# Forgetting attention on one core: where silu of the gate runs, and where ScalarE loads its function table

## The chip, the cores and the metric

The kernel runs on one core of a Trainium2 chip. A core has TensorE (PE in the profile, with its weight loads as PEld), VectorE (DVE), ScalarE (ACT), GpSimd (POOL) and a queue engine that issues transfers (SP). The metric is device time in microseconds. Before the change it was 2946.18 us, the median of three runs (2945.17 to 2953.4).

## The reference, cut to what matters

The program is a first block of two layers, followed by a second block of two mixers. The last mixer is forgetting attention over 512 positions with 16 heads of 64, and this change is inside it:

```python
def fox_mixer(h, w_in, f_bias, qn_w, kn_w, w_out):
    proj = h @ w_in
    q, k, v, z, f = jnp.split(proj, [...], axis=-1)
    q = rmsnorm(q.reshape(shp), qn_w) * FOX_HEAD_DIM ** -0.5
    k = rmsnorm(k.reshape(shp), kn_w)
    log_f = jax.nn.log_sigmoid(f + f_bias)
    cum = jnp.cumsum(log_f, axis=1)
    o = forgetting_attention(q, k, v, cum).reshape(B, S, FOX_WIDTH)
    o = o * jax.nn.silu(z)
    return o.astype(h.dtype) @ w_out

def forgetting_attention(q, k, v, cum):   # for each block of 128 queries
    logits = jnp.einsum('bqhd,bkhd->bhqk', q_b, k)
    logits = logits + (c_b[..., :, None] - cum_k[..., None, :])
    p = jax.nn.softmax(jnp.where(mask, logits, -jnp.inf), axis=-1)
    return jnp.einsum('bhqk,bkhd->bqhd', p, v)
```

So each pair of heads needs four projections (q, k, v, z) of 1024 by 128, two root mean square norms, a causal softmax, its product with v, and a product with silu(z).

## The kernel before, in words

Activations lie transposed (features on partitions, 512 positions in a row). Every weight block (1024 by 128) is loaded in float32, rounded by ScalarE into `w_hi` (L237), and its rest is formed by VectorE in `w_lo` (L243). A projection of one block is 24 products on TensorE (L255), three for each of 8 slices of the depth.

Forgetting attention handles two heads in a **turn**, eight turns in all, numbered 0 to 7 here. `fox_turns` writes turns 0 to 5 as a loop of three trips with two turns each, and turns 6 and 7 behind it. A turn has 16 steps n, and each engine has its own hand-written order of them. In the same steps the projections and norms of the **next** pair are made (`fox_next_pe`, `fox_next_act`, `fox_next_dve`), so that turn j also prepares turn j+1. Turn 7 has no next pair; it mixes in products of the output projection (L2608 to L2610) instead. The preparation of turn 0 stands alone ahead of the loop. Engines meet only through semaphores, and each engine executes its own list strictly in that order.

What stands in the steps:

- n = 0 to 7: TensorE makes the scores of unit n, s0 to s7 (L2564 to L2566, two heads times four query blocks); VectorE takes the row maximum (L2707, L2709); ScalarE computes ex0 to ex7, the exponentials with the row sums (L2644); VectorE inverts the sums (L2697) and GpSimd scales the probabilities (L2731). The scores of unit u wait for exponential u-2, which frees the bank.
- n = 8 to 15: TensorE transposes the probabilities, t0 to t7 (L2574); ScalarE copies each result out of the bank, pc0 to pc7 (L2652); TensorE multiplies it with v, v0 to v7 (L2582), one step later.
- Every n: a quarter of a projection of the next pair (six products, L255). At n = 7 and n = 10 TensorE also sums squares of q and of k with a product with ones (L2457), which waits for ScalarE's squares (L2472, at n = 5 and n = 9).
- ScalarE for the next pair: `w_hi` at n = 0, 4, 8, 12; at n = 8 the logarithm and exponential that give the inverse root for q (L2478, L2480), at n = 11 the same for k; at n = 10 four half copies of q (L2487, L2490), at n = 13 two of k (L2495), at n = 15 a copy of the turned v (L2498).
- The end of a turn: VectorE multiplies the attention with silu(z) (L2703, after v3 and v7), ScalarE rounds the product into `h_hi` (L2659), VectorE forms `h_lo` (L2718).

ScalarE computes nonlinear functions from a loaded table set. Silu needs another set than the exponential and the logarithm, and the compiler puts an ACT_TABLE_LOAD ahead of a function that the present set lacks; `preload_act_table_set` puts one where it is written. Copies and squares need none. In the kernel before, silu of the present pair's z stands right behind pc0 (L2655), and ahead of each of the two logarithms stands a preload of the set that has logarithm and exponential (L2476).

Of the kernel before, what the change touches and what calls it, by code (L numbers as in the profile page):

```python
# [108 lines left out]
def first_and_second_block(nc, a, out):  # L109

    with ExitStack() as ctx:
        def sem(name):
            return ctx.enter_context(nc.semaphore(name))
# [589 lines left out]
        class Gla:  # L703
# [3 lines left out]
            u = [tile(f"gla_u{n}", (21, 30, 31, 32)[n]) for n in range(4)]  # L707
# [14 lines left out]
            act = Steps(sem("gla_act"), ["zb0", "az0", "zb1", "az1", "ez0", "ez1", "lz0", "lz1"]  # L722
                        + [f"{n}{m}" for m in range(2) for n in ("eq", "ek", "e_mid", "e_all", "e_end")]
                        + ["vt0", "vt1", "kt0", "kt1", "vt2", "vt3"] + [f"{n}{h}" for p in (0, 2) for n in ("sq", "oc", "ln") for h in (p, p + 1)] + [f"rs{h}" for h in range(4)]
                        + [f"silu{h}" for h in range(4)] + ["hi7", "hi6", "hi5", "hi4", "hi0", "hi1", "hi2", "hi3"])
# [406 lines left out]
        class Dsa:  # L1132
# [23 lines left out]
            act = Steps(sem("dsa_act"), ["sin1", "abs1", "cos1", "sin0", "abs0", "cos0"]  # L1156
                        + [n for d in range(12) for n in [f"rl{d + 1}{h}" for h in range(IDX_HEADS) if d < TT - 1]
                           + [f"sw_{r}" for r in dsa_swaps[d]]] + ["vt0", "vt1", "vt2", "vt3"])
# [6 lines left out]
        class DsaAtt:  # L1165

            units, groups = range(DSA_UNITS), range(DSA_UNITS // DSA_GROUP)
# [3 lines left out]
            act = Steps(sem("dsa_att_act"), [f"ex{u}" for u in range(2)]  # L1171
                        + [n for u in units for n in [f"ex{u + 2}"] * (u + 2 < DSA_UNITS) + [f"pc{u}"]
                           + [f"hi{u // DSA_GROUP - 1}"] * (u >= DSA_GROUP and u % DSA_GROUP == 1)] + [f"hi{DSA_UNITS // DSA_GROUP - 1}"])
# [354 lines left out]
        class Gdn:  # L1528
# [12 lines left out]
            zs = [tile(f"gdn_zs{h}", 18 + h) for h in range(2)]  # L1541
# [6 lines left out]
            XT, X, F, m, V1, F2, V, CY = Pw[0], Pw[1], W2[0], W2[1], W3[1], W5[0], W5[1], W3[0]  # L1548
# [3 lines left out]
            raw, x, ax, ex = W1[0], W2[0], W3[0], Pw[0]  # L1552
# [48 lines left out]
        class GdnNext:  # L1601

            pe = Steps(sem("gdn_next_pe"), ["sum_q", "sum_k"])
            act = Steps(sem("gdn_next_act"), ["cw0", "cw1", "cs0", "cw2", "cs1", "sq_q", "sq_k", "cw3", "ss_q", "ss_k", "cs2", "cs3",
                                              "ln_q", "ln_k", "rs_q", "rs_k", "eg_0", "eg_1", "dec_0", "dec_1"])
# [3 lines left out]
        class GdnOut:  # L1609

            act = Steps(sem("gdn_out_act"), both(["ln", "rs", "hi"]))
            dve = Steps(sem("gdn_out_dve"), both(["on", "o", "lo"]))

        class GdnTurn:
# [7 lines left out]
            act = Steps(sem("gdn_act"), ["kc", "vc_0", "vc_1", "fa", "fb", "c", "f2a", "y", "bt", "ct"]  # L1622
                        + [n for t in range(TT) for n in both([f"vn{t}"])] + both(["sq", "oc"]))
# [746 lines left out]
        class Fox:  # L2370
            b0, t0 = BASE["fox"]
            f, x, ax, ex, all_ones, cum = (tile(f"fox_{n}", 31 + k) for k, n in enumerate(("f", "x", "ax", "ex", "all_ones", "cum")))
# [20 lines left out]
        class FoxTurn:  # L2393

            units = range(2 * TT)
            pe = Steps(sem("fox_turn_pe"), [f"s{u}" for u in units] + [n for u in units for n in [f"t{u}"] + [f"v{u - 1}"] * (u > 0)] + ["v7"])
            act = Steps(sem("fox_turn_act"), [f"ex{u}" for u in units] + [n for u in units for n in [f"pc{u}"] + ["zs"] * (u == 0)] + ["hi"], 2 * 8 + 2)
            dve = Steps(sem("fox_turn_dve"), [n for u in units for n in [f"mx{u}", f"nm{u}"] + [f"ri{u - 1}"] * (u > 0)] + ["ri7", "ga_0", "ga_1", "lo"], 1)
            pool = Steps(sem("fox_turn_pool"), [f"pn{u}" for u in units])

# [63 lines left out]
        def fox_next_act(act, n, j, m, i, scored):  # L2464

            F, N = Fox, FoxNext
            if n % 4 == 0:
                split_hi(act, fox_block(m, n // 4) + AHEAD, i, 8)
            if n in (5, 9):
                k = (5, 9).index(n)  # L2470
                act.wait_ge(*fox_taken(m, k, i))
                act.activation(F.sq[k][:], (F.q, F.k)[k][:], ACT.Square).then_inc(*N.act.done(f"sq_{'qk'[k]}"))  # L2472
            if n in (8, 11):

                k = (8, 11).index(n)
                act.preload_act_table_set("natural_log_exp_and_others")  # L2476
                act.wait_ge(*N.pe.after(f"sum_{'qk'[k]}", j))
                act.activation(F.sd[k][:], fox_bank(m, k)[:], ACT.Ln, bias=eps_c, scale=1.0 / FOX_DH).then_inc(*N.act.done(f"ln_{'qk'[k]}"))  # L2478
                act.wait_ge(*N.act.after(f"ln_{'qk'[k]}", j))
                act.activation(F.sd[k][:], F.sd[k][:], ACT.Exp, scale=-0.5).then_inc(*N.act.done(f"rs_{'qk'[k]}"))  # L2480
            if n == 10:
                act.wait_ge(*N.dve.after("n_q", j))
                if scored:
                    act.wait_ge(*scored)
                for h in range(2):
                    r = fox_rows(h)[0]
                    act.activation(F.q2[h][r, :], F.q[r, :], ACT.Copy).then_inc(*N.act.done(f"q2_{h}"))  # L2487
                for h in range(2):
                    r, other = fox_rows(h)
                    act.activation(F.q2[h][other, :], F.q[r, :], ACT.Copy).then_inc(*N.act.done(f"qq_{h}"))  # L2490
            if n == 13:
                act.wait_ge(*N.dve.after("n_k", j))
                for h in range(2):
                    r = fox_rows(h)[0]
                    act.activation(F.k2[h][r, :], F.k[r, :], ACT.Copy).then_inc(*N.act.done(f"k2_{h}"))  # L2495
            if n == 15:
                act.wait_ge(*N.pe.after("vt", j))
                act.activation(F.v_tok[m % 2][:], fox_bank(m, 2)[:], ACT.Copy).then_inc(*N.act.done("vt"))  # L2498
# [121 lines left out]
        def fox_act(act, after):  # L2620
            F, N, H, s = Fox, FoxNext, FoxTurn, Fox.act
            act.sem_inc(H.act.sem, H.act.lead)
            project_act(act, F.b0, 1)
            act.wait_ge(tile_free, BANKS + F.t0 + 1)
            r = slice(0, P)
            act.activation(F.x[r, :], F.f[r, :], ACT.Identity, bias=nfox_b[r, :]).then_inc(*s.done("x"))
            act.activation(F.ax[r, :], F.f[r, :], ACT.Abs, bias=nfox_b[r, :]).then_inc(*s.done("ax"))
            act.wait_ge(*s.after("ax"))
            act.preload_act_table_set("natural_log_exp_and_others")
            act.activation(F.ex[r, :], F.ax[r, :], ACT.Exp, scale=-1.0).then_inc(*s.done("ex"))  # L2630
            act.wait_ge(*s.after("ex"))
            act.activation(F.ax[r, :], F.ex[r, :], ACT.Ln, bias=1.0).then_inc(*s.done("ln"))
            for n in range(16):
                if n == 8:
                    act.wait_ge(*F.dve.after("ones"))
                fox_next_act(act, n, 0, 0, 0, None)

            def turn(j, i, m, last):
                for n in range(16):
                    if not last and n < 8:  # L2640
                        fox_next_act(act, n, j + 1, m + 1, i, H.pe.after("s7", j))
                    if n < 8:
                        act.wait_ge(*H.dve.after(f"nm{n}", j))
                        act.activation(fox_p(n), bank[4 + n % 2][:, 0:fox_keys(n)], ACT.Exp, bias=nmax[:, n:n + 1],  # L2644
                                       scale=FOX_DH ** -0.5, accum_out=rowsum[:, n:n + 1]).then_inc(*H.act.done(f"ex{n}"))
                    else:
                        u = n - 8
                        act.wait_ge(*H.pe.after(f"t{u}", j))
                        if u >= 2:
                            act.wait_ge(*H.pe.after(f"v{u - 2}", j))  # L2650
                        w = T - u % TT * P
                        act.activation(F.pT[u % 2][:, 0:w], bank[4 + u % 2][:, 0:w], ACT.Copy).then_inc(*H.act.done(f"pc{u}"))  # L2652
                        if u == 0:
                            act.wait_ge(*fox_taken(m, 3, i))
                            act.activation(F.z[m][:], F.z[m][:], ACT.Silu).then_inc(*H.act.done("zs"))  # L2655
                        if not last:
                            fox_next_act(act, n, j + 1, m + 1, i, H.pe.after("s7", j))
                act.wait_ge(*H.dve.after("ga_1", j))
                act.activation(h_hi[:, col(j)], F.gated[:], ACT.Copy).then_inc(*H.act.done("hi"))  # L2659
            fox_turns(act, turn)  # L2660
            down_act(act, F.b0 + FOX_P, KT, after)

# [399 lines left out]
```

## Time and profile before

| what | value |
|---|---|
| median of three runs | 2946.18 us |
| the profiled execution | 2946.31 us |
| its span, first to last instruction | 2944.5 us |
| mean granted TensorE clock | 0.981 |
| TensorE busy | 2813.8 us |
| VectorE busy | 1616.8 us |
| ScalarE busy | 1259.0 us |
| GpSimd busy | 621.9 us |

Times in rows are microseconds from the span's start. "Idle before <-releaser" in brackets is how long the engine stood still before the instruction, and what ended that. A granted clock of 1.00 is TensorE's full 2.4 GHz, 0.50 is 1.2 GHz. The preparation of turn 0 begins near 2570 us, turn 0 begins at 2600.60 us and the last turn ends near 2902 us; the output projection and the final norm follow.

### The profile page before, as it was taken

What the parts mean: (1) busy time and instruction counts of PE and PEld (TensorE: products, weight loads), DVE (VectorE), ACT (ScalarE), POOL (GpSimd) and SP (SyncE); (2) the same over time, 40 slices, a digit from 0 to 9 for tenths busy, and PEclk for the clock granted to TensorE, in tenths of its full rate; (3) what the DMA queues carried; (4) which work ended last, traced back from release to release, by engine and by line L of the source; (5) the groups of instructions that cost most, each with busy time, mean ns of one, the idle gap of its engine ahead of it and who ended that gap; (6) DMA issues with size and microseconds to landing.
All of it is one profiled execution on the core that took longest, in us unless ns stands there. A gap on an engine that the chain in (4) does not pass through costs nothing.

```text
span 2944.5 us, 41200 instructions
## 1 busy us (share of the span) xinstructions
PE 2813.8 (96%) x14333; PEld 2279.4 (77%) x14333; DVE 1616.8 (55%) x2484; ACT 1259.0 (43%) x1853; POOL 621.9 (21%) x594
## 2 busy tenths in 40 slices
PE   7999999999999999999899999979999999799998
PEld 5888877788888878886678788857888887576667
DVE  4444345544433665336845653266777777565554
ACT  4443242444422333233443332255555555466664
POOL 2000103100001550013533510233333333122222
PEclk9999999999999999999899999999999999899999
DMA  4333332233333563332114643321222222122212
GB/s 120 103 95 96 92 79 72 72 99 94 91 98 89 168 174 113 93 91 72 43 51 136 177 130 94 94 72 51 66 66 65 66 65 55 44 65 52 55 50 65
DMA packets 485303, 255.65 MB, mean 87 GB/s; under 512 B 18819, under 2 KB 479398, under 8 KB 485174
## 3 DMA queue, kind: packets, MB, share of 16 engines
q1 hardware_dynamic: 483856, 253.25, 30.1%
q8 instruction: 81, 1.33, 0.2%
q10 hardware_dynamic: 1318, 0.69, 0.1%
q14 instruction: 48, 0.39, 0.0%
HBM read 251.77 MB, written 2.13 MB: 86 GB/s over the span
## 4 chain that ended last, share of the span: by engine, by line
PE 76%; DVE 9%; ACT 5%; issue 4%; POOL 4%; ACTq 0%; DVEq 0%; DMA 0%; POOLq 0%
PE bank L255 58%; PE bank L1727 2%; ACT w_hi L237 2%; POOL sumsq L587 1%; PE bank L2582 1%; POOL ada_sum L587 1%; DVE dsa_work L1458 1%; DVE prod L683 1%; PE bank L1758 1%; DVE ada_hi L573 1%; PE bank L1825 1%; PE bank L1760 1%; PE bank L1759 1%; DVE w_lo L243 1%; DVE small L1456 1%
## 5 line engine op out<-in xcount | busy, mean ns | idle before, releaser
L255 PE MATMUL bank<-x_hi,w_hi 128*128 128x512 f32 x2328 | 958.4, 412 | 20.3 <-DVE w_lo L243 9.0
L255 PE MATMUL bank<-x_hi,w_lo 128*128 128x512 f32 x2328 | 915.4, 393 | 0.0
L255 PE MATMUL bank<-x_lo,w_hi 128*128 128x512 f32 x2328 | 914.5, 393 | 0.0
L243 DVE TENSOR_TENSOR w_lo<-w_raw,w_hi 128x1024 fp32r<-128x1024 f32 x430 | 550.2, 1281 | 661.8 <-ACT w_hi L237 655.1
L237 ACT ACTIVATE w_hi<-w_raw 128x1024 fp32r<-128x1024 f32 x430 | 451.1, 1052 | 426.5 <-PE bank L255 388.4
L255 PEld LDWEIGHTS bank<-x_hi,w_hi 128*128 128x128 f32 x2328 | 442.2, 190 | 131.3 <-issue 21.5
L255 PEld LDWEIGHTS bank<-x_hi,w_lo 128*128 128x128 f32 x2328 | 441.3, 190 | 95.6
L255 PEld LDWEIGHTS bank<-x_lo,w_hi 128*128 128x128 f32 x2328 | 442.7, 190 | 92.5 <-issue 9.1
L400 POOL TENSOR_TENSOR sumsq<-sumsq,sq 128x512 f32<-128x512 f32 x54 | 91.9, 1703 | 1318.5 <-ACT sq L386 1317.1
L255 PE MATMUL bank<-h_hi,w_hi 128*128 128x512 f32 x768 | 298.9, 389 | 1.6 <-DVE h_lo L1483 1.6
L255 PE MATMUL bank<-h_lo,w_hi 128*128 128x512 f32 x768 | 298.8, 389 | 0.0
L255 PE MATMUL bank<-h_hi,w_lo 128*128 128x512 f32 x768 | 298.8, 389 | 0.0
L659 ACT ACTIVATE h_hi<-prod 128x512 f32 x88 | 55.7, 632 | 387.9 <-DVE prod L683 387.9
L255 PEld LDWEIGHTS bank<-h_hi,w_hi 128*128 128x128 f32 x768 | 144.2, 188 | 31.8 <-issue 1.8
L255 PEld LDWEIGHTS bank<-h_hi,w_lo 128*128 128x128 f32 x768 | 144.2, 188 | 29.9
L255 PEld LDWEIGHTS bank<-h_lo,w_hi 128*128 128x128 f32 x768 | 144.2, 188 | 29.7
L656 ACT ACTIVATE gate_s<-gate_s 128x512 f32<-128x512 f32 x88 | 55.7, 632 | 184.5 <-DVE gate_s L675 184.5
L680 DVE TENSOR_TENSOR prod<-bank,rstd 128x512 f32<-128x512 f32 x88 | 60.6, 689 | 85.9 <-PE bank L255 85.9
L686 DVE TENSOR_TENSOR h_lo<-prod,h_hi 128x512 f32 x88 | 62.4, 709 | 82.3 <-ACT h_hi L659 82.3
L587 POOL TENSOR_TENSOR sumsq<-sumsq,ada_hi 128x512 f32<-128x512 f32 x48 | 62.1, 1294 | 159.9 <-DVE ada_hi L573 159.9
L2731 POOL TENSOR_TENSOR fox_p<-fox_p,small 128x128 f32<-128x128 f32 (+1 forms) x64 | 59.0, 921 | 99.4 <-DVE small L2697 98.6
L683 DVE TENSOR_TENSOR prod<-prod,gate_s 128x512 f32<-128x512 f32 x88 | 77.0, 875 | 4.6
(450 smaller groups left out, 3663.4 us busy)
## 6 DMA issues: line engine op xcount, KB each, us to landing
w_raw<-in_ffn_wi_dram SPq DMA_DIRECT2D x176, 512.0 KB, 3.8
w_raw<-in_ffn_wo_dram SPq DMA_DIRECT2D x64, 512.0 KB, 3.6
w_raw<-in_ada_w_dram SPq DMA_DIRECT2D x48, 512.0 KB, 4.8
w_raw<-in_a_w_in_dram SPq DMA_DIRECT2D x48, 512.0 KB, 3.9
w_raw<-in_b_w_in_dram SPq DMA_DIRECT2D x32, 512.0 KB, 4.0
w_raw<-in_ffn_wo_dram SPq DMA_DIRECT2D x32, 384.0 KB, 3.1
w_raw<-in_even_w_in_dram SPq DMA_DIRECT2D x16, 512.0 KB, 4.0
w_raw<-in_a_w_out_dram SPq DMA_DIRECT2D x16, 512.0 KB, 3.6
```

The costliest lines, as they stand in the source:

```text
L237: act.activation(w_hi[b % SPLIT][:], w_raw[raw % RAW][:], ACT.Copy).then_inc(w_hi_done, 1)
L243: dve.tensor_tensor(w_lo[s][:], w_raw[raw_of(b) % RAW][:], w_hi[s][:].bitcast(F32), ALU.subtract).then_inc(w_lo_done, 1)
L255: mm = pe.matmul(out, lhs[:, w], rhs(kt), start=first and kk == 0 and m == 0, stop=last and kk == len(kts) - 1 and m == 2)
L400: pool.tensor_tensor(sumsq[:], sumsq[:], sq[k % 2][:], ALU.add).then_inc(sum_added, 1)
L587: pool.tensor_tensor(dst, x, y, ALU.add).then_inc(ada_added, 1)
L656: act.activation(gate_s[s][:], gate_s[s][:], ACT.Silu).then_inc(silu_done, 1)
L659: act.activation(h_hi[:, col(i * 2 + 2 * turn0 + s)], prod[s][:], ACT.Copy).then_inc(h_hi_done, 1)
L680: dve.tensor_tensor(prod[s][:], bank[(t0 + o + 1) % BANKS][:], rstd[:], ALU.mult).then_inc(tile_free, 1)
L683: dve.tensor_tensor(prod[s][:], prod[s][:], gate_s[s][:], ALU.mult).then_inc(prod_done, 1)
L686: dve.tensor_tensor(h_lo[:, h], prod[s][:], h_hi[:, h].bitcast(F32), ALU.subtract).then_inc(h_ready, 1)
L1727: mm = pe.matmul(out[:, c * INV_PART:(c + 1) * INV_PART], lhs(c), rhs(c), start=True, stop=True)
L2731: pool.tensor_tensor(fox_p(u), fox_p(u), rinv[:, u:u + 1].to_broadcast([P, fox_keys(u)]), ALU.mult).then_inc(*H.pool.done(f"pn{u}"))
```

## The change

Two edits on ScalarE, and the list of its signals that goes with them. The preload inside `fox_next_act` is taken out, and one preload of the same set is written at the head of every turn. Silu of z moves from behind pc0 (n = 8) to behind pc5 (n = 13), and it now comes after that step's work for the next pair. What is computed stays the same.

```diff
-            act = Steps(sem("fox_turn_act"), [f"ex{u}" for u in units] + [n for u in units for n in [f"pc{u}"] + ["zs"] * (u == 0)] + ["hi"], 2 * 8 + 2)
+            act = Steps(sem("fox_turn_act"), [f"ex{u}" for u in units] + [n for u in units for n in [f"pc{u}"] + ["zs"] * (u == 5)] + ["hi"], 2 * 8 + 2)
...
                 k = (8, 11).index(n)
-                act.preload_act_table_set("natural_log_exp_and_others")
                 act.wait_ge(*N.pe.after(f"sum_{'qk'[k]}", j))
...
             def turn(j, i, m, last):
+
+                act.preload_act_table_set("natural_log_exp_and_others")
                 for n in range(16):
...
                         act.activation(F.pT[u % 2][:, 0:w], bank[4 + u % 2][:, 0:w], ACT.Copy).then_inc(*H.act.done(f"pc{u}"))
-                        if u == 0:
+                        if not last:
+                            fox_next_act(act, n, j + 1, m + 1, i, H.pe.after("s7", j))
+                        if u == 5:
                             act.wait_ge(*fox_taken(m, 3, i))
                             act.activation(F.z[m][:], F.z[m][:], ACT.Silu).then_inc(*H.act.done("zs"))
-                        if not last:
-                            fox_next_act(act, n, j + 1, m + 1, i, H.pe.after("s7", j))
```

Only ScalarE's list changes. In these rows `fox_pT` is a copy pc, `fox_sd` the logarithm and exponential of a norm, `fox_sq` a square, `fox_p` an exponential ex; ISA and REGISTER_ALU rows are bookkeeping of semaphores and loop counters. In the first turn of the loop's body, behind pc0 at n = 8, ScalarE's list held this before:

```order
L2655 ACT_TABLE_LOAD
L2655 ACTIVATE fox_z_255<-fox_z_255 128x512 [waits tile_free]
L235 REGISTER_ALU
L236 REGISTER_ALU [waits w_loaded0]
L237 ACTIVATE w_hi_56<-w_raw_52 128x1024 [waits block_done]
L2476 ACT_TABLE_LOAD
L2477 ISA
L2478 ACTIVATE fox_sd_261<-bank,small 128x512 [waits fox_next_pe]
L2479 ISA
L2480 ACTIVATE fox_sd_261<-fox_sd_261 128x512 [waits fox_next_act]
L2648 REGISTER_ALU
L2652 ACTIVATE fox_pT_266<-bank 128x384 [waits fox_turn_pe]
```

In the changed kernel, the same place beginning with pc0 itself:

```order
L2653 ACTIVATE fox_pT_265<-bank 128x512 [waits fox_turn_pe]
L235 REGISTER_ALU
L236 REGISTER_ALU [waits w_loaded0]
L237 ACTIVATE w_hi_56<-w_raw_52 128x1024 [waits block_done]
L2476 ISA
L2477 ACTIVATE fox_sd_261<-bank,small 128x512 [waits fox_next_pe]
L2478 ISA
L2479 ACTIVATE fox_sd_261<-fox_sd_261 128x512 [waits fox_next_act]
L2649 REGISTER_ALU
L2653 ACTIVATE fox_pT_266<-bank 128x384 [waits fox_turn_pe]
L2471 REGISTER_ALU
L2472 ACTIVATE fox_sq_260<-fox_k 128x512 [waits tile_free]
```

Both table loads and silu are gone from between pc0 and the square of k; the rest keeps its order.

At n = 13, behind the two half copies of k, the list went straight to pc6 before:

```order
L2495 ACTIVATE fox_k_0_248<-fox_k 64x512 [waits fox_next_dve]
L2495 ACTIVATE fox_k_1_249<-fox_k 64x512
L2648 REGISTER_ALU
L2650 REGISTER_ALU [waits fox_turn_pe]
L2652 ACTIVATE fox_pT_265<-bank 128x256 [waits fox_turn_pe]
L2648 REGISTER_ALU
```

In the changed kernel a table load and silu stand there:

```order
L2494 ACTIVATE fox_k_0_248<-fox_k 64x512 [waits fox_next_dve]
L2494 ACTIVATE fox_k_1_249<-fox_k 64x512
L2657 REGISTER_ALU
L2658 ACT_TABLE_LOAD
L2658 ACTIVATE fox_z_255<-fox_z_255 128x512 [waits tile_free]
L2649 REGISTER_ALU
L2651 REGISTER_ALU [waits fox_turn_pe]
L2653 ACTIVATE fox_pT_265<-bank 128x256 [waits fox_turn_pe]
```

The pair that left n = 8 comes back in front of pc6.

At the border of two turns, the rounding into `h_hi` was followed by `w_hi` and ex0 before:

```order
L2659 ISA [waits fox_turn_dve]
L2659 ACTIVATE h_hi<-fox_gated 128x512
L236 REGISTER_ALU [waits w_loaded2]
L237 ACTIVATE w_hi_58<-w_raw_54 128x1024 [waits block_done]
L2643 ISA
L2644 ACTIVATE fox_p_263,small<-bank,small 128x128 [waits fox_turn_dve]
```

In the changed kernel:

```order
L2660 ISA [waits fox_turn_dve]
L2660 ACTIVATE h_hi<-fox_gated 128x512
L2639 ACT_TABLE_LOAD
L236 REGISTER_ALU [waits w_loaded2]
L237 ACTIVATE w_hi_58<-w_raw_54 128x1024 [waits block_done]
L2644 ISA
L2645 ACTIVATE fox_p_263,small<-bank,small 128x128 [waits fox_turn_dve]
```

A table load now stands in front of `w_hi` and ex0 of the new turn. In a turn there were three loads, and there are now two; in the preparation of turn 0 the two loads of L2476 are gone, and turn 0 has one at its head.

## Rows read from the trace of the kernel before

**Rows 1.** The page, part 1: busy time, share of the span, instructions.

```profile
PE 2813.8 (96%) x14333; PEld 2279.4 (77%) x14333; DVE 1616.8 (55%) x2484; ACT 1259.0 (43%) x1853; POOL 621.9 (21%) x594
```

**Rows 2.** Waits from 2600 to 2902 us: total, times, longest.

```profile
PE bank L2457 <- ACT fox_sq L2472: 22.2, 7, 3.2
...
PEld bank L2582 <- ACT fox_pT L2652: 4.3, 12, 0.5
```

**Rows 3.** Timeline of TensorE: first score product of turns 0, 2, 3, 4, 7.

```profile
2600.60 0.32 PE L2564 MATMUL bank<-fox_k,fox_q 128*128 128x128 f32 x1 [1.13 <-DVE fox_k L2538]
...
2679.00 0.22 PE L2564 MATMUL bank<-fox_k,fox_q 128*128 128x128 f32 x1
...
2717.27 0.22 PE L2564 MATMUL bank<-fox_k,fox_q 128*128 128x128 f32 x1
...
2757.28 0.22 PE L2564 MATMUL bank<-fox_k,fox_q 128*128 128x128 f32 x1
...
2876.09 0.22 PE L2564 MATMUL bank<-fox_k,fox_q 128*128 128x128 f32 x1
```

**Rows 4.** Timeline of ScalarE in turn 2: start us, us, engine, line, operation.

```profile
2695.04 0.60 ACT L2652 ACTIVATE fox_pT<-bank 128x512 f32<-128x512 f32 x1 [0.18 <-PE bank L2574]
2695.66 1.28 ACT L2655 ACT_TABLE_LOAD   x1
2696.95 0.63 ACT L2655 ACTIVATE fox_z<-fox_z 128x512 f32<-128x512 f32 x1
2697.49 1.04 ACT L237 ACTIVATE w_hi<-w_raw 128x1024 fp32r<-128x1024 f32 x1
2698.55 1.28 ACT L2476 ACT_TABLE_LOAD   x1
2699.85 0.69 ACT L2478 ACTIVATE fox_sd<-bank,small 128x512 f32<-128x512 f32 x1
2700.57 0.63 ACT L2480 ACTIVATE fox_sd<-fox_sd 128x512 f32<-128x512 f32 x1
2701.10 0.47 ACT L2652 ACTIVATE fox_pT<-bank 128x384 f32<-128x384 f32 x1
2701.47 0.62 ACT L2472 ACTIVATE fox_sq<-fox_k 128x512 f32<-128x512 f32 x1
```

**Rows 5.** Timeline of TensorE in the same turn.

```profile
2698.57 0.39 PE L255 MATMUL bank<-x_hi,w_lo 128*128 128x512 f32 x1
...
2702.14 1.13 PE L2457 MATMUL bank<-fox_sq,ones 128*128 128x512 f32 x2 [3.18 <-ACT fox_sq L2472]
```

**Rows 6.** Windows of TensorE: stretch, length, busy (instructions), granted clock, DMA share, GB/s.

```profile
2663.00:2663.50 0.50, 0.50 (x3) 0.50 0.49 148
2702.50:2703.00 0.50, 0.50 (x2) 1.00 1.15 348
2857.50:2858.00 0.50, 0.00 (x0) 0.51 0.52 150
```

**Rows 7.** Timeline of ScalarE, later in turn 2.

```profile
2706.64 1.28 ACT L2476 ACT_TABLE_LOAD   x1
...
2713.11 0.38 ACT L2652 ACTIVATE fox_pT<-bank 128x256 f32<-128x256 f32 x1 [0.83 <-PE bank L2574]
```

**Rows 8.** Head of turn 3: ScalarE, then the third score product.

```profile
2717.04 0.63 ACT L2659 ACTIVATE h_hi<-fox_gated 128x512 f32 x1 [1.03 <-DVE fox_gated L2703]
...
2719.07 0.37 ACT L2644 ACTIVATE fox_p<-bank,small 128x128 f32<-128x128 f32 x1 [0.45 <-DVE small L2709]
...
2720.73 0.34 PE L2564 MATMUL bank<-fox_k,fox_q 128*128 128x384 f32 x1
```

**Rows 9.** Before turn 0: TensorE at the second sum, and VectorE.

```profile
2589.65 1.12 PE L2457 MATMUL bank<-fox_sq,ones 128*128 128x512 f32 x2 [1.68 <-ACT fox_sq L2472]
...
2587.10 1.21 DVE L243 TENSOR_TENSOR w_lo<-w_raw,w_hi 128x1024 fp32r<-128x1024 f32 x1
```

**Rows 10.** Last turn: TensorE at the second value product.

```profile
2891.89 0.91 PE L2582 MATMUL bank<-fox_pT,fox_v_tok 128*128 128x384 f32 x2 [0.22 <-ACT fox_pT L2652]
```

## The prediction

> **What bounds the kernel now.** I read the page first: TensorE is busy for 2813.8 us of a span of 2944.5 us [rows 1]. Busy is not the same as necessary, but it says that a change on ScalarE counts only where TensorE stands still for ScalarE. So the second view is the list of waits over the stretch of the eight turns. One line outweighs the others there: TensorE waited 7 times for a square before a sum of squares, 22.2 us in total, 3.2 us the longest [rows 2]. Seven is the number of turns that prepare a next pair. The next line is much smaller: 12 waits of the weight load for a copy pc, 4.3 us.
>
> Third, the timelines of the two engines in turn 2. TensorE starts the last of its six products of n = 10 at 2698.57 and the sum of squares of k at 2702.14 [rows 5]. A full-rate product is followed by the next start 0.23 us later, so the sum could have started at 2698.80: the delay is 3.34 us. ScalarE has no gap at all from pc0 (2695.04) to the square of k (2701.47 to 2702.09) [rows 4]. This is one chain of nine instructions, and the square is its last. Three of the nine are what this change takes out.
>
> Fourth, the length of the turns and the granted clock. The first score product of turn 2 starts at 2679.00, of turn 3 at 2717.27, of turn 4 at 2757.28 [rows 3]: turn 2 takes 38.27 us and turn 3 takes 40.01 us, with the same work. The clock explains it. After the wait in turn 1, TensorE is granted 0.50 (1.2 GHz) in a stretch in which it is busy throughout; in turn 2, after an equally long wait, it keeps 1.00; in turn 6 the clock falls while it still waits [rows 6]. What TensorE did before each fall was nothing, for some 3 us. Turns 0 to 6 take 2876.09 - 2600.60 = 275.49 us together. Seven at 38.27 would be 267.89, so the low clock costs 7.6 us over them.
>
> **The change, part by part.**
>
> Chain from pc0 to the square of k. Removed are a load and silu (2695.66 to w_hi at 2697.49) and a load (2698.55 to the logarithm at 2699.85) [rows 4]. Rebuilt from the same rows: instructions of ScalarE overlap by about 0.1 us, as the exponential at 2700.57 (0.63) and pc1 at 2701.10 do. w_hi then starts at 2695.04 + 0.60 - 0.10 = 2695.54, the logarithm 0.95 later at 2696.49, the exponential 0.72 later at 2697.21 (it keeps its wait for the logarithm), pc1 at 2697.74, the square at 2698.11, ending at 2698.73. TensorE wants it at 2698.80. So the wait goes whole, with 0.07 us to spare; I count 3.35 us a turn less about 0.05 for the semaphore, 3.3 us. Simple subtraction of the rows gives 1.83 + 1.30 = 3.13 us, and I keep that as the lower end. Over seven turns: 23.1 us (21.9 to 23.4).
>
> Can the earlier instructions start earlier? w_hi needs a weight block that has landed, and a buffer freed by the block that TensorE ended at n = 7, before pc0. The logarithm needs the sum over q, also of n = 7. pc1 needs t1, which TensorE does before n = 10. None of them is late.
>
> Low clock. If a 3.2 us wait is what lets the clock fall, no turn has one any more, and the 7.6 us come back. The ends are 0 and 7.6; I take 7.5, since outside these waits I see no fall inside the turns.
>
> Second load of L2476, at n = 11 (2706.64) [rows 7]. It delays the second logarithm and all behind it on ScalarE by 1.3 us, up to pc4. v4 is one of the 12 short waits for a copy, 4.3 / 12 = 0.36 us each [rows 2]. I take 0.3 us a turn, 2.1 us in seven; ends 0 and 4.3.
>
> Silu at n = 13. A load of 1.28 and silu of 0.63 now stand before pc6. Ahead of them ScalarE is 1.3 us earlier by the load that went, and pc6 waited 0.83 us for its transposes anyway [rows 7]. That is 2.1 us of lead against 1.9 us of new work, so pc6 is late by at most 0.3 us where a little of the lead is lost at pc4 and pc5. v6 comes a step later, after six products (6 x 0.23 = 1.4 us). Queued behind the pair are pc6, pc7 and the copy of v; the gate product on VectorE also waits for silu now, but it runs only after that engine's two subtractions for k. I take 0; the ends are 0 and 0.3 us a turn, 2 us.
>
> Load at the head of a turn. It stands between h_hi (2717.04) and w_hi, with ex0 behind (2719.07, after 0.45 us idle) [rows 8]. ex0 becomes late by 1.30 - 0.45 = 0.85 us. The one who waits is the third score product; it needs ex0, which ended with its row sum about 0.46 us after its start, at 2719.53, and it starts at 2720.73. Slack 1.2 us, use 0.85: nothing, with 0.35 to spare. VectorE's inverse of the first sum is pushed by some 0.4 us, and w_lo behind it. The ends are 0 and 0.5 us a turn, 3.5 us.
>
> The Trainium skill bears on this place. "ScalarE: Activation LUTs", section "What ACT_TABLE_LOAD costs", says that a switch of sets costs the load of about 1.28 us and a drain of about 1.38 us. The rows agree on the load and show no drain: 0.02 us lie between the end of pc0 and the load, and 0.01 between the load and silu [rows 4]. By that rule the sum would be some 7 us smaller (rival B); the measured rows decide, and I go by 1.3.
>
> Preparation of turn 0. Both loads of L2476 vanish. TensorE waited 1.68 us at the second sum [rows 9] and 1.13 us at the first score [rows 3], 2.8 us together, which bounds the gain. The first norm of q is not free to move by all of 1.3 us, because VectorE is in w_lo until 2588.31 (2587.10 + 1.21) [rows 9]; I take 2.2 us, ends 1.3 and 2.8. The load at the head of turn 0 falls where ScalarE idles.
>
> Turn 7. Without load and silu before pc1, its value product does not wait (0.22 us and its late start [rows 10]): 0.4 us, ends 0 and 0.5. Silu before pc6 here delays the first gate product, which is not the last.
>
> **Sum**: 23.1 + 7.5 + 2.1 + 2.2 + 0.4 = 35.3 us. The profiled execution took 2946.31 us, 0.13 above the median, so the time is 2946.3 - 35.3 = 2911.0 us. The work of a plain turn falls from 38.27 to about 34.7 us.
>
> **The rivals.**
>
> A, the clock falls anyway. Some other short stillness may be enough once turns are shorter, or the wait at 2902 near the end may now meet a fall. For: in the rows equal waits gave a fall in one turn and none in the next, so a fall is not decided by the wait alone. Against: the dense stretches never show one. Cost up to 7.5 us: 2918.5.
>
> B, a new wait at the head or at pc6. The loads stand before ex0 and before silu, and my slack at the head is only 0.35 us. If both ends of those terms come true: 3.5 + 2 = 5.5 us, 2916.5. The strongest form is that a switch costs the length of the load once more before it: ex0 is then 0.85 + 1.30 = 2.15 us late against a slack of 1.2, which is 0.95 x 7 = 6.7 us, 2917.7. Against it stand the 0.02 us between pc0 and its load [rows 4]. The page of the Trainium skill named above states this form.
>
> C, the sum of squares goes free only by half, since something else in its chain is late once ScalarE is early (the copy of k by VectorE, a weight block). 1.65 x 7 = 11.5 us less, and the low clock stays in about half the turns: about 2926.
>
> D, slower. The square is not what TensorE waits for: another input of the sum arrives at the same moment, and nothing is gained there. Then ScalarE's new load at the head and the pair at n = 13 are on the path of each turn: 8 x (1.30 + 1.91) = 25.7 us on top, 2972. It decides only if no slack exists at the head, where I read 1.2 us, and ScalarE stood without a gap up to the very square that released TensorE. The rows speak against both halves.
>
> E, the loads that were removed return, placed by the compiler, and nothing happens: 2946. The order of the built program shows two per turn instead of three, so this is nearly excluded.
>
> **How the numbers follow.** Forecast (2906 to 2916) 0.70; A 0.11; B 0.09; C 0.06; D 0.02; E 0.02. The time is 2911. The lower end of the range adds the favourable ends: 0.3 at the sums, 2.2 at the copies, 0.6 before turn 0 and a little shorter turns otherwise, 2906; 2905 stands. The upper end takes in A and B and part of their combination, 2922. Beyond lie C, D and E. This kernel's measurement tells about 0.3%, some 9 us, from no change. All of forecast, A, B and C are more than that below 2946: faster 0.96, same 0.02, slower 0.02.
>
> **What would show it.** In the profile after: the wait of L2457 for the square of k gone from the list of waits or below 0.3 us each; turns of about 34.7 us from first score to first score, all alike; granted clock 1.00 throughout turns 0 to 7; the third score product of a turn still without a wait; pc6 starting with little or no idle time and v6 not waiting. The forecast is wrong if turns still come in two lengths, if the third score waits for ex0, or if the sum of squares waits for more than 1 us.

## The result, and the profile after

The changed kernel takes 2911.57 us, the median of four runs (2910.64 to 2913.47). The kernel before takes 2948.44 us in the runs beside it (2945.17 to 2953.4). The ratio is 0.9874, with a 95% interval of 0.9861 to 0.9888: 1.26% faster. The prediction was 2911.0 us. The four runs of the kernel before lie in two groups (2945.17 and 2946.18; 2950.7 and 2953.4), so its median falls between them. The profiled execution from which the prediction subtracts, 2946.31 us, is of the lower group.

The profiled execution took 2910.64 us, with a span of 2908.8 us. Part 1 of its page:

```profile
PE 2801.8 (96%) x14333; PEld 2272.5 (78%) x14333; DVE 1611.7 (55%) x2484; ACT 1247.7 (43%) x1845; POOL 624.4 (21%) x594
```

ScalarE has eight instructions less, which are the loads (16 removed, 8 added) [rows 1]. TensorE has the same 14333 products and 12 us less busy time.

The first score products of turns 0, 2, 3, 4 and 7, which answer to [rows 3] (in this kernel the line is L2563), in the timeline of TensorE:

```profile
2595.87 0.32 PE L2563 MATMUL bank<-fox_k,fox_q 128*128 128x128 f32 x1 [0.40 <-DVE fox_k L2537]
...
2665.74 0.22 PE L2563 MATMUL bank<-fox_k,fox_q 128*128 128x128 f32 x1
...
2700.43 0.22 PE L2563 MATMUL bank<-fox_k,fox_q 128*128 128x128 f32 x1
...
2735.46 0.22 PE L2563 MATMUL bank<-fox_k,fox_q 128*128 128x128 f32 x1
...
2839.48 0.22 PE L2563 MATMUL bank<-fox_k,fox_q 128*128 128x128 f32 x1
```

Turn 2 takes 34.69 us (38.27 before), turn 3 35.03 us (40.01 before), and turns 0 to 6 together 243.61 us (275.49 before). The chain of turn 1 on ScalarE, which answers to [rows 4]:

```profile
2646.69 0.60 ACT L2653 ACTIVATE fox_pT<-bank 128x512 f32<-128x512 f32 x1 [0.19 <-PE bank L2573]
2647.19 1.05 ACT L237 ACTIVATE w_hi<-w_raw 128x1024 fp32r<-128x1024 f32 x1
2648.14 0.68 ACT L2477 ACTIVATE fox_sd<-bank,small 128x512 f32<-128x512 f32 x1
2648.85 0.63 ACT L2479 ACTIVATE fox_sd<-fox_sd 128x512 f32<-128x512 f32 x1
2649.39 0.47 ACT L2653 ACTIVATE fox_pT<-bank 128x384 f32<-128x384 f32 x1
2649.76 0.62 ACT L2472 ACTIVATE fox_sq<-fox_k 128x512 f32<-128x512 f32 x1
```

From pc0 to the end of the square of k it is now 3.69 us instead of 7.05. TensorE at the sum of squares, against [rows 5]:

```profile
2650.24 0.40 PE L255 MATMUL bank<-x_hi,w_lo 128*128 128x512 f32 x1
2650.47 1.09 PE L2457 MATMUL bank<-fox_sq,ones 128*128 128x512 f32 x2
```

The sum (L2457) starts 0.23 us after the last product: there is no wait. The list of waits from turn 0 to the end of turn 7, against [rows 2]:

```profile
PEld bank L2581 <- ACT fox_pT L2653: 3.1, 8, 0.4
...
PE bank L2607 <- DVE h_lo L2719: 2.2, 1, 2.2
...
PEld bank L2457 <- ACT fox_sq L2472: 1.6, 7, 0.2
```

The 22.2 us of TensorE's own waits at L2457 are gone; what is left there is 1.6 us at the weight load, mostly hidden. The granted clock over turns 0 to 6, and in a stretch right behind turn 7:

```profile
2595.87:2839.48 243.61, 243.26 (x1149) 1.00 0.23 61
...
2866.00:2866.50 0.50, 0.50 (x2) 0.50 0.00 0
```

The same view of the kernel before, over its turns 0 to 6:

```profile
2600.60:2876.09 275.49, 252.96 (x1149) 0.97 0.20 54
```

Before, TensorE was busy for 252.96 of 275.49 us at a mean clock of 0.97; now it is busy for 243.26 of 243.61 us at 1.00, with the same 1149 instructions. So the turns are now TensorE's own work. The second row of the first of these fences is new and tells of something else: behind the last turn TensorE waits 2.2 us for `h_lo` (L2607 in the waits), and the clock is 0.50 after it in this execution.

Where the 35.7 us between the two spans went, by the starts of the same instructions:

| stretch | before | after | difference |
|---|---|---|---|
| start to the first activation of forgetting attention (untouched code) | 2573.14 | 2570.59 | -2.55 |
| preparation of turn 0, to its first score | 27.46 | 25.28 | -2.18 |
| turns 0 to 6 | 275.49 | 243.61 | -31.88 |
| turn 7 to the end | 68.41 | 69.32 | +0.91 |

The first row is no effect of the change: over the fourteen profiles of this document, whose code is the same up to there, that point lies anywhere from 2570.25 to 2573.61, and in a later profile of the changed kernel at 2572.00. The last holds the low clock behind turn 7: in that later profile it stays at full clock, and the stretch is 67.89 us, 0.52 less than before. So what the change itself moves is 2.18 + 31.88 + 0.52 = 34.6 us at full clock behind turn 7, and 33.2 us with the low clock of this execution.

### The profile page after: what moved, and what is told of

It reads as the page before. It is cut to its first block, busy times and chain, and to the rows that moved or that the text cites. A ratio compares the mean times of both kernels' runs of the same rounds, so it can differ in the third digit from the quotient of the medians.

```text
span 2908.8 us, 41195 instructions
## 1 busy us (share of the span) xinstructions
PE 2801.8 (96%) x14333; PEld 2272.5 (78%) x14333; DVE 1611.7 (55%) x2484; ACT 1247.7 (43%) x1845; POOL 624.4 (21%) x594
## 4 chain that ended last, share of the span: by engine, by line
PE 78%; DVE 9%; ACT 4%; POOL 4%; issue 4%; ACTq 0%; DVEq 0%; DMA 0%; POOLq 0%
PE bank L255 59%; PE bank L1727 2%; ACT w_hi L237 2%; POOL sumsq L587 1%; PE bank L2581 1%; POOL ada_sum L587 1%; DVE dsa_work L1458 1%; DVE prod L683 1%; PE bank L1758 1%; DVE w_lo L243 1%; DVE ada_hi L573 1%; PE bank L1825 1%; PE bank L1760 1%; PE bank L1759 1%; DVE small L1456 1%
```

## Experiments: how much of the chain, and what the clock does

**The old loads stay, only silu leaves the chain.** In `fox_next_act` of the changed kernel:

```diff
                 k = (8, 11).index(n)
+                act.preload_act_table_set("natural_log_exp_and_others")
                 act.wait_ge(*N.pe.after(f"sum_{'qk'[k]}", j))
```

> The changed kernel with both old loads kept ahead of the logarithms (n = 8 and n = 11), so of the change only silu and its load have left the chain. My theory: each instruction in the chain from pc0 to the square of k delays TensorE by its own length. The load at n = 8 is back, so the sum of squares of k waits about 1.3 us in each of 7 turns, v4 and v6 wait 0.3 us each again, and the preparation of turn 0 loses 2.2 us: 9.1 + 4 + 2.2 = 15 us over the changed kernel's 2911.6, near 2926. The waits of 1.3 us leave the clock at 1.00. Rival A, the clock falls whatever the length of the wait: about 7 us more, 2933. Rival, silu alone was the whole change and the other loads were covered: 2912.

Measured: 2924.57 us (2923.45 to 2926.08), ratio to before 0.9931 (0.9914 to 0.9947). TensorE's waits for the square over turns 0 to 6, and the window over them:

```profile
PE bank L2457 <- ACT fox_sq L2472: 8.6, 7, 1.2
```

```profile
2601.07:2856.31 255.24, 246.32 (x1149) 1.00 0.21 58
```

The wait is 1.23 us in each of 7 turns: one load, at its own length. The clock stays at 1.00, so a wait of this length brings no low clock with it here. The preparation of turn 0 is back at 27.46 us. Both rivals fall, and the theory is off by 1.4 us: v4 comes 0.27 us late again, as expected, but v6 does not, which I had priced at 0.3 us a turn. Against the kernel before beside it (2944.88) it is 20.3 us less: taking silu with its load out of the chain is more than half of the gain, low clock included, and the other loads are the rest.

**Two and three loads in the chain.** Again in the changed kernel, in the turns that prepare a next pair; the kernel with two has the first two of these, that with three has all:

```diff
+                if n == 8 and scored:
+                    act.preload_act_table_set("natural_log_exp_and_others")
                 act.wait_ge(*N.pe.after(f"sum_{'qk'[k]}", j))
...
+                if n == 8 and scored:
+                    act.preload_act_table_set("natural_log_exp_and_others")
                 act.wait_ge(*N.act.after(f"ln_{'qk'[k]}", j))
                 act.activation(F.sd[k][:], F.sd[k][:], ACT.Exp, scale=-0.5)...
+                if n == 8 and scored:
+                    act.preload_act_table_set("natural_log_exp_and_others")
```

> The changed kernel with two extra table loads in the chain of n = 8, one ahead of the logarithm and one between it and the exponential, in the 7 turns that prepare a next pair. My theory: the wait for the square of k comes back with 2 x 1.3 - 0.05 = 2.5 us, and pc6 is some tenths late: 7 x 2.6 = 18 us, 2930, if the clock stays at 1.00. If waits of 2.5 us let the clock fall as those of 3.2 us did, up to 7 us more, 2937. Rival with a drain at each load (a load costs 2.6 us): 7 x 5.2 = 36 us, 2948.

> As the last one with a third extra load, between the exponential and pc1. My theory: a wait of 3.85 us in 7 turns, 27 us, 2939, and the clock falls after it in each turn or nearly each (before: 4 of 7 with waits of 3.2 us), 1.7 us each: 12 us more, 2951. If the falls had another cause than the wait, they stay away and it is 2939.

Measured: 2934.44 us with two (ratio 0.9967, 0.9955 to 0.998), between the two times I had given (2930 and 2937), and 2952.94 us with three (1.0028, 1.0017 to 1.0038), where I had 2951. With two:

```profile
PE bank L2457 <- ACT fox_sq L2472: 17.5, 7, 2.5
```

```profile
2597.64:2863.33 265.69, 247.88 (x1149) 0.99 0.21 56
```

With three:

```profile
PE bank L2457 <- ACT fox_sq L2472: 27.5, 7, 3.9
```

```profile
2598.01:2882.53 284.52, 256.66 (x1148) 0.95 0.19 52
```

The waits are 2.5 us and 3.9 us, that is 1.3 to 1.4 us more for each load: nothing beyond the load itself is to be seen. TensorE loses a little more than the list counts as a wait: in turn 2 the sum of squares starts 1.39, 2.66 and 3.34 us later than in the changed kernel with one load, with two, and in the kernel before, for waits of 1.24, 2.50 and 3.18 us. In half-microsecond windows, the clock of the kernel with two is 0.50 behind 2 of its 7 waits, and its other turns take 37.3 to 37.7 us. With three it is 0.50 behind all 7. Together with the experiment above and the kernel before this gives a row of the same wait in four lengths:

| kernel | wait, us | turns 0 to 6 with low clock | us of turns 0 to 6 |
|---|---|---|---|
| changed | 0 | 0 of 7 | 243.6 |
| one load | 1.2 | 0 of 7 | 255.2 |
| two loads | 2.5 | 2 of 7 | 265.7 |
| before (two loads and silu) | 3.2 | 4 of 7 | 275.5 |
| three loads | 3.9 | 7 of 7 | 284.5 |

Lengthening this wait alone, in a kernel that is otherwise the same, brings the low clock back: the wait causes it. Which of several equally long waits it follows, the length does not settle. A stretch of it cost 1.36 to 1.44 us in turns 1, 3 and 5 of the kernel before and up to 1.7 us in the kernel with two loads; some came twice in a row, and part of a stretch may fall into the wait itself, where it costs nothing.

**The second load alone.** In the kernel before:

```diff
                 k = (8, 11).index(n)
-                act.preload_act_table_set("natural_log_exp_and_others")
+                if n == 8:
+                    act.preload_act_table_set("natural_log_exp_and_others")
```

> The kernel before, without the load ahead of the second logarithm (n = 11) and nothing else. My theory: this load is covered but for 0.3 us at v4 in 7 turns and about 1 us in the preparation of turn 0, some 3 us: 2943 to 2945 against 2946 to 2948. The wait of 3.2 us for the square of k stays, and turns still come in two lengths about 1.7 us apart. Rival, every load counts with its full 1.3 us wherever it stands: 8 x 1.3 = 10 us, 2937.

Measured: 2949.25 us, ratio to before 1.0008 (0.9998 to 1.0017), no difference. Neither forecast came true. The runs lie in two groups, 2941 to 2943 (three) and 2948 to 2953 (seven). The profile is of the upper one:

```profile
PE bank L2457 <- ACT fox_sq L2472: 22.2, 7, 3.2
```

```profile
2596.42:2880.49 284.07, 261.59 (x1149) 0.93 0.19 52
```

The waits are those of before to the tenth, 22.2 us in 7. But low clock follows all seven, five times in a double stretch, and turns 0 to 6 take 284.07 us instead of 275.49. The preparation of turn 0 is 26.2 us, 1.3 less than before, as expected. So the saved 0.3 us a turn can't be read from this time, since low clock behind three more waits costs more than that. It can be read from the traces: at v4 of turn 0 the weight load waited 0.25 us for the copy before (at 2631.52) and does not wait here (at 2628.70), and TensorE gains 0.27 us between the product before v4 and the one behind it. The lower group (2941.07 to 2942.81) lies 2 to 4 us under the kernel before beside it (median 2944.88), where I had expected some 3 us, but no profile of that group was taken.

**The kernel before, once more.** The same file.

> The kernel before, once more with a profile. Its times lie in two groups, 2943 to 2946 and 2951 to 2954. My theory: the groups differ by how many stretches of low clock follow the waits of 3.2 us; the first profile (2946) had low clock after 4 of 7 waits. If this execution is of the upper group, low clock follows 6 or 7 of the 7 waits, and turns 0 to 6 take 4 to 8 us more than 275.5; if it is of the lower group, they take 273 to 276. Rival: the groups come from elsewhere, and the turns take the same 275.5 in both.

Measured: 2945.37 us, ratio 0.9999 (0.9988 to 1.001), all runs in the lower group. Turns 0 to 6 take 275.48 us with low clock behind the same four waits as in the first profile. The upper group of this kernel (2951 to 2954, seen in runs beside the result and beside two groups of experiments) was not caught in a profile, so which waits the low clock follows there is not shown. The mean granted clock of each run is on record: 0.976 to 0.978 in the nine such runs beside the experiments, and 0.979 to 0.982 in all 45 of the lower group. A drop of 0.003 over 2950 us is 9 us of full-rate time lost, enough for the 7 us between the groups.

## Experiments: the slack where the work was moved to

**A second load at the head of the turn.** In the changed kernel, between w_hi and ex0:

```diff
+                    if n == 0:
+                        act.preload_act_table_set("natural_log_exp_and_others")
                     if n < 8:
                         act.wait_ge(*H.dve.after(f"nm{n}", j))
```

> The changed kernel with a second load at the head of a turn, between w_hi and ex0 (it can't be had in turn 7, where no w_hi stands between). My theory: ex0 ended 0.85 us before the third score product of turn 2 in the changed profile, so 1.3 us more lets TensorE wait 0.45 us in 6 turns (turn 0 is covered): 3 us, near 2914.5. Rival B with a drain at a load: 1.8 us in 6 turns, 11 us, 2923.

Measured: 2917.6 us (2916.55 to 2918.81), ratio to before 0.989 (0.9875 to 0.9905), against 2910.63 for the changed kernel beside it: 7 us where I expected 3. From its list of waits (the score line is L2563, the inverse of a row sum L2700):

```profile
PE bank L2563 <- ACT fox_p L2647: 4.2, 6, 0.8
...
DVE small L2700 <- ACT fox_p L2647: 14.9, 14, 1.6
```

The third score product of turns 1 and 2:

```profile
2635.13 0.45 PE L2563 MATMUL bank<-fox_k,fox_q 128*128 128x384 f32 x1 [0.84 <-ACT fox_p L2647]
...
2671.17 0.44 PE L2563 MATMUL bank<-fox_k,fox_q 128*128 128x384 f32 x1 [0.48 <-ACT fox_p L2647]
```

TensorE stands still for 0.48 us in turns 2 and 4, as forecast, but for 0.84 us in turns 1, 3 and 5 and 0.73 in turn 6: the slack I had used is that of turn 2, and in turns 1, 3 and 5 of the changed kernel it is less (in turn 3, ex0 ends at 2703.40 and the third score starts at 2703.88: 0.5 us). The idle time is also not the whole price. Against the same turn of the changed kernel TensorE is 0.75 us late behind this pair of products in turn 2 and 1.11 us in turn 3, which is 0.27 us more than the wait each time; the later scores are not delayed further. Turns 1 to 6 took 6.2 us more. The rival with a drain asked for 11 us and falls.

**A load behind silu, ahead of pc6.**

```diff
                             act.activation(F.z[m][:], F.z[m][:], ACT.Silu).then_inc(*H.act.done("zs"))
+                            act.preload_act_table_set("natural_log_exp_and_others")
```

> The changed kernel with one more load behind silu, ahead of pc6. My theory: pc6 ended 0.9 us before v6, so v6 waits 0.4 us in each turn: 3 us, near 2914.5. Rival, the copies have slack enough and nothing happens: 2911.6. Rival with a drain: 2.6 - 0.9 = 1.7 us in 8 turns, 2925.

Measured: 2915.18 us (2913.39 to 2915.57), ratio to before 0.988 (0.9862 to 0.9898), 4.6 us over the changed kernel beside it. The waits over turns 0 to 6:

```profile
PE bank L2581 <- ACT fox_pT L2653: 2.9, 7, 0.4
```

0.41 us in each turn, as read from the slack of 0.9 us; the last turn adds 1.0 us. In the profiles another 1.1 us of the difference lies ahead of turn 0, in code that both share. The moved pair stands with 0.9 us to spare where it is. This load switches back from the set of silu, so it is also a test of the rival with a drain, which asked for 2925 us: in turn 1 silu ends at 2663.10, the load runs from 2663.12 to 2664.40 and pc6 starts at 2664.41. That rival falls.

**Silu at the very end, behind pc7 and the copy of v.**

```diff
-            act = Steps(sem("fox_turn_act"), [f"ex{u}" for u in units] + [n for u in units for n in [f"pc{u}"] + ["zs"] * (u == 5)] + ["hi"], 2 * 8 + 2)
+            act = Steps(sem("fox_turn_act"), [f"ex{u}" for u in units] + [n for u in units for n in [f"pc{u}"] + ["zs"] * (u == 7)] + ["hi"], 2 * 8 + 2)
...
-                        if u == 5:
+                        if u == 7:
```

> The changed kernel with silu and its load behind pc7 and the copy of v (n = 15) instead of behind pc5. My theory: silu then ends about 2 us after v7, the gate products and h_hi come 2.7 us later, the load at the head and ex0 with them, and the third score product, whose slack is 0.85 us, waits 1.8 us in turns 1 to 7: 13 us, near 2924. The sum of squares stays free and the clock stays at 1.00 inside the turns. Rival, any place outside the chain of n = 8 is as good: 2911.

Measured: 2935.06 us (2933.05 to 2936.05), ratio to before 0.9957 (0.9943 to 0.9972): 24 us over the changed kernel where I expected 13. The direction is right and the rival ("any place will do") falls. The waits for ex0, one in each of turns 1 to 7, and VectorE at the end of turn 1:

```profile
PE bank L2563 <- ACT fox_p L2645: 16.4, 7, 2.6
```

```profile
2672.89 0.68 DVE L2704 TENSOR_TENSOR fox_gated<-bank,fox_z 64x512 f32<-64x512 f32 x1 [4.61 <-ACT fox_z L2658]
2673.50 0.67 DVE L2504 COPY fox_z<-bank 128x512 f32<-128x512 f32 x1
2674.20 0.69 DVE L2704 TENSOR_TENSOR fox_gated<-bank,fox_z 64x512 f32<-64x512 f32 x1
```

The wait is 2.2 to 2.6 us in turns 1 to 6 and 1.6 us in turn 7, not 1.8. The first gate product (L2704) waits for silu, and queued behind it on VectorE are the copy of z and the second gate product, so h_hi comes 3.3 us later, not 2.7. As above, each wait costs 0.27 us more than its idle time. The clock did not stay at 1.00 inside the turns, as I had expected: it is 0.50 behind the wait of 2.61 us in turn 1 (39.32 us, against 37.92 for turn 3), which adds 1.4 us. Together turns 0 to 6 take 17.9 us more than in the changed kernel. The rest is at the end: behind turn 7 nothing covers silu, TensorE waits 4.35 us for `h_lo` instead of 2.17, and low clock follows. From the start of turn 7 to the end this kernel takes 74.34 us, 6.5 more than the changed kernel beside it, which had no low clock there.

## Experiments: a version that beats both

**The fourth block of the output projection begun early.** What the profile after leaves is the wait of 2.2 us behind turn 7. This kernel splits the weights of the fourth output block on ScalarE and VectorE during turn 7, and multiplies seven of its eight slices before TensorE needs `h_hi` and `h_lo` of turn 7:

```diff
-            for q in range(FOX_EARLY):
+            output(FOX_EARLY, range(KT - 1))
+            for q in range(FOX_EARLY + 1):
                 output(q, (KT - 1,))
-            for q in range(FOX_EARLY, KT):
+            for q in range(FOX_EARLY + 1, KT):
                 output(q, range(KT))
...
+                        if last and u == 2:
+                            split_hi(act, F.b0 + FOX_P + AHEAD)
...
+                    elif n == 11:
+                        split_lo(dve, F.b0 + FOX_P + AHEAD)
```

(`down_act` and `down_dve` leave out their first split in turn.)

> The changed kernel once more, as the comparison for the runs beside it: 2911 to 2913, turns of 34.6 to 35.1 us. Whether the clock falls after the wait of 2.2 us behind turn 7 is open, as it did in one profile and not in the other.

> The changed kernel, with TensorE's wait behind turn 7 (2.2 us for h_lo) filled: the fourth block of the output projection is split during turn 7, and its first seven slices are multiplied ahead of the last slice of blocks 0 to 2. My theory: the 2.2 us go, about 0.4 us come back as a wait for the split of block 4, and the clock can't fall there (1.7 us in the changed kernel's profile): 2 to 3.5 us less, 2908 to 2910. Rival: the waits for the splits of blocks 4 and 5 take all of it, 2911.5 or more.

Measured: 2910.63 us for the changed kernel (2910.31 to 2911.78; ratio to before 0.9867, 0.985 to 0.9885; a little under the 2911 to 2913 I had given), 2910.03 us with the block begun early (2907.52 to 2911.92; 0.9865, 0.9846 to 0.9883). The spread was too wide to tell them apart, so both ran again:

> The kernel with the fourth output block split and begun early, once more. Its profile showed 3.2 us less behind the start of turn 7 than the changed kernel, its median only 0.6 us less, within the spread. If the gain is in the time too, the median lies 2 to 3.5 us under that of the changed kernel beside it; if the profile misled, they are equal within 1 us.

> The changed kernel once more, beside the kernel with the fourth output block begun early: 2910.5 to 2912.5 us, the spread of its earlier runs.

Measured: 2908.65 us with the block begun early (2907.42 to 2909.66; ratio 0.987, 0.9853 to 0.9887), 2911.16 us for the changed kernel (2910.54 to 2912.84; 0.988, 0.9863 to 0.9896). This time no run of the one reaches a run of the other, and the difference of the medians is 2.5 us. The only wait of TensorE behind turn 7 until the end of the projection:

```profile
2871.93 0.47 PE L2607 MATMUL bank<-h_hi,w_hi 128*128 128x512 f32 x1 [0.52 <-DVE w_lo L243]
```

0.52 us for the split of the next block instead of 2.2 us. From the start of turn 7 to the end it is 66.23 us, against 67.89 for the changed kernel beside it, which had no low clock there, and 69.51 in its first repeat, which had. In the profiles the gain is 1.7 us, and another 1.4 to 1.6 us in those executions in which the clock would have fallen; 0.95 us more of the difference between these two profiles lies ahead of turn 0, in code that both share. The medians differ by 0.6 us in the first pair of kernels and by 2.5 in the second, so the size in time is no better known than that. It is under 0.1% of the whole.

## Why the prediction was right

The mechanism, the place and the size came out, 2911.0 against 2911.57 us. Part of that agreement is luck: the profiled execution had already gained 2.55 us in code that the change does not touch, and lost 1.4 us to a low clock behind turn 7. Without both, the change moved 34.6 us where the sum has 35.3. The forecast also starts from an execution of the lower group; from one of the upper group (2951 to 2954) the same sum would have given 2916 to 2919 us. Step by step:

- **Sum of squares, 3.3 us a turn.** Right. The wait is 0, and the six instructions left of the chain of nine run as rebuilt. Lined up product by product, the sum of squares of turn 2 starts 3.34 us earlier in its turn. One, two and three loads put in again gave waits of 1.2, 2.5 and 3.9 us.
- **Copies, 0.3 us a turn.** Right in size: turns without low clock went from 38.27 to 34.69, 3.58 us, where 3.3 + 0.3 stood, and the step at v4 is 0.27 us, in the kernel without the second load too. The time of that kernel does not show it, because low clock decides over more there. The source I had named was read loosely: of the 12 short waits only the three at v4 (0.24 to 0.25 us each, in the turns without low clock) belong to this term; seven are at v7, 0.33 to 0.41 us each, and are still there after the change.
- **Low clock, 7.5 us.** Right in kind, mis-sized by 0.7 us: turns 0 to 6 gave 31.88 us, of which 7 x 3.58 = 25.1 is the work just named, which leaves 6.8. I had taken all turns as equal at 38.27; turns 1 and 3, each in front of the loop's jump back, are 0.35 to 0.4 us longer also at full clock (35.10 and 35.03 against 34.69). That the jump is the reason was not tested.
- **Preparation of turn 0, 2.2 us.** Measured 2.18. VectorE's `w_lo` was indeed what limited it: in the changed kernel the norm of q (2585.67) follows it without a gap, where it waited 0.80 us for ScalarE before.
- **Head of the turn, 0.** Right, and with a little more to spare: I had 0.35 us left of the slack, and it is 0.9 us in turn 2 and 0.5 in turns 1, 3 and 5.
- **Silu at n = 13, 0.** Right. In turn 1 the load and silu stand at 2659.91 to 2661.84, and v6 does not wait:

```profile
2659.91 1.28 ACT L2658 ACT_TABLE_LOAD   x1
...
2661.21 0.63 ACT L2658 ACTIVATE fox_z<-fox_z 128x512 f32<-128x512 f32 x1
...
2661.74 0.37 ACT L2653 ACTIVATE fox_pT<-bank 128x256 f32<-128x256 f32 x1
...
2664.95 0.63 ACT L2660 ACTIVATE h_hi<-fox_gated 128x512 f32 x1 [0.71 <-DVE fox_gated L2704]
...
2665.60 1.28 ACT L2639 ACT_TABLE_LOAD   x1
...
2666.90 1.06 ACT L237 ACTIVATE w_hi<-w_raw 128x1024 fp32r<-128x1024 f32 x1
...
2667.86 0.35 ACT L2645 ACTIVATE fox_p<-bank,small 128x128 f32<-128x128 f32 x1
```

The same fence shows the head of turn 2 on ScalarE: h_hi, the load, w_hi and ex0 without a gap. TensorE's third score product stands behind it without a wait:

```profile
2669.20 0.34 PE L2563 MATMUL bank<-fox_k,fox_q 128*128 128x384 f32 x1
```

- **Turn 7, 0.4 us.** 0.52 in a profile at full clock; in the first one the low clock behind it turned this into +0.91. Rival A named that place ("the wait at 2902 near the end may now meet a fall"), and it happened in two of three profiles of the changed kernel.
- **The page's price of a switch.** By the Trainium skill, "ScalarE: Activation LUTs", section "What ACT_TABLE_LOAD costs", a drain of about 1.38 us belongs to each switch; it doesn't say on which side of the load. The traces do not agree. The loads that repeat the present set cost 1.3 us in the experiments, and the two that switch sets in the changed kernel have 0.01 to 0.02 us of idle time around them in the rows above. The load put behind silu switches sets as well and cost no more. In none of the fourteen profiles has a load behind 2600 us more than 0.02 us of idle time ahead of it.

## What to carry to other kernels

Look for the one instruction that another engine waits for, and count everything that stands before it on its own engine since the last time that engine was idle; work that nobody needs yet (silu of a gate, a table load) belongs behind it, at a place whose slack was read from the profile of the same turn that is tightest. A wait of TensorE of 2.2 to 3.9 us can cost more than itself, since the clock may be at half rate afterwards, and how often it is varies from one run to the next; so a small saving in a kernel with such waits hardly shows in its time until the waits are gone, and is looked for in the trace, by lining up the same products. The two experiments whose cost I forecast too small (3 for 7 us, 13 for 24 us) were short for several reasons: slack read in one turn and less in others, 0.27 us lost beyond each idle time, what stood queued on VectorE behind the waiting gate product, and low clock behind the new waits. When an instruction is made late, follow its queue on each engine that waits for it, in the tightest turn and in the last one.

## What the runs showed of the hardware

- The same wait in lengths of 1.2, 2.5, 3.2 and 3.9 us had low clock (0.50, 1.2 GHz) behind 0, 2, 4 and 7 of 7 waits. Equal waits of 3.2 us gave it behind 4 of 7 in two profiles of one kernel and behind 7 of 7 in a kernel that differs by one covered load. The single wait of 2.17 us behind turn 7 stands in eleven of the profiles, always of the same length, and has low clock behind it in five: in two of the three of the changed kernel, and in those with a second load at the head, with a load behind silu and with three loads. It has none in both of the kernel before. So length alone does not decide it.
- With no such waits inside the turns the spread of the times shrinks: 2910.3 to 2913.5 us over 12 runs of the changed kernel, against 2942.5 to 2954.0 over 58 runs of the kernel before, 11 of them in the upper group.
- A table load of the set that is already active takes the full 1.28 us, as one that switches sets does.
- A wait costs TensorE a little more than its idle time: 0.16 us at the sum of squares, 0.27 us at the third score product.
